# Gate and up products of 12 of 22 tiles by seven half-size products (Strassen, one level) on normalised x

## The chip, the cores and the metric

The kernel runs on 1 core of one Trainium2 chip. The metric is the device time of one execution in microseconds (us), the median of several runs. Five engines work side by side and meet at semaphores: PE (TensorE, matmuls), DVE (VectorE), ACT (ScalarE), POOL (GpSimd) and SP (SyncE, which issues the weight loads). Each engine works through its own program strictly in order.

## The reference, cut to what matters

A two-layer encoder trunk on x of 512 tokens by 1024 features, all in float32. It has four feed-forward blocks, and between them mixers (convolution and attention in layer 0, a short gated convolution in layer 1) that the change does not touch.

```
def rmsnorm(x, g):
    y = xf * lax.rsqrt(jnp.mean(xf * xf, axis=-1, keepdims=True) + EPS)
    return (y * g.astype(jnp.float32)).astype(x.dtype)

def swiglu(x, w_gate, w_up, w_down):
    return (jax.nn.silu(x @ w_gate) * (x @ w_up)) @ w_down

x = x + FFN_RES * swiglu(rmsnorm(x, ffn1_norm[layer]), ffn1_w_gate[layer],
                         ffn1_w_up[layer], ffn1_w_down[layer])
```

`w_gate` and `w_up` are 1024 x 2816, which is 22 tiles of 128 columns; `w_down` is 2816 x 1024.

## The kernel before

**Layout.** Activations are kept transposed: 128 features on the partitions, 512 tokens along the free dimension. x times the norm's gain is held as `xg_hi` and `xg_lo`, 8 feature tiles of 128 x 512 each. Every float32 operand is held as a high part (rounded to the matmul's float32r) and a low part (the rest), and one product is three matmuls: high by high, high by low, low by high (`product`, L1288 to 1292).

**A feed-forward block** is a "pair" phase and a "resid" phase (the product with `w_down`). The pair phase has 44 units: gate and up of tile 0, gate and up of tile 1, and so on. A unit is 8 products over the feature tiles into one PSUM bank, 24 matmuls of 128x128 by 128x512 (`projection`, L1305). Four units make a group; the units of a group use banks 0 to 3. Group 0 is written out, the others are a loop.

**What a unit needs.** SP loads its 512 KB into one of four `raw` slots. ACT copies it to `w_hi` (L637, one instruction over 128x1024) once the unit two before is finished on PE, because there are two `w_hi` and `w_lo` slots; DVE subtracts (L950) to make `w_lo`. The next load into a raw slot waits for the `w_lo` made from it.

**What a tile needs afterwards.** DVE multiplies the gate bank by `rstd` (L1025), ACT applies silu (L688), POOL multiplies by `rstd` again for the up side (L516), DVE multiplies by the up bank (L1032, `hid`), ACT copies to `h_hi` (L693), DVE subtracts to `h_lo` (L1035). The normalisation of x is thus applied to the products, not to x, and `rstd` is only computed while the first units run: PE sums the squares after unit 0, ACT takes a logarithm and an exponential, DVE finishes (L962 to 964).

**Order.** Nothing plans at run time. The order on each engine is what the functions named `pair` and `group` write out; an engine that waits holds up all that stands behind it.

Of the kernel before, what the change touches and what calls it, by code (L numbers as in the profile page):

```python
# [28 lines left out]
P = 128  # L29
BANKS = 8  # L30
EPS = 1e-6
MASKED = -1.0e30


# [15 lines left out]
def plan(phases):  # L50
    unit = pair = gate_act = h = 0
    for n, ph in enumerate(phases):
        ph.unit0, ph.pair0, ph.act0, ph.h0, ph.pair_end = unit, pair, gate_act, h, pair
        unit += ph.units
        if ph.kind == "pair":
            pair += ph.units // 2
            if ph.gate != "none":
                gate_act += ph.units // 2
            if ph.gate == "silu":
                h += ph.units // 2  # L60
        if n:
            phases[n - 1].next = ph
    return phases


def trunk(nc, t_in, out):
# [67 lines left out]
    raw = own("raw", [P, 4, SLOT])  # L134
    w_hi, w_lo = own("w_hi", [P, 2, SLOT], f32r), own("w_lo", [P, 2, SLOT], f32r)
    rstd = own("rstd", [P, S])
# [4 lines left out]
    hid = at("hid", [P, S], f32, HID)  # L141
    sq = own("sq", [P, 2, S])
    sq_sum = own("sq_sum", [P, S])
    cum = own("cum", [P, S])
    WIDE = 2 * P
# [21 lines left out]
    rough, corr = at("rough", [P, S], f32, ACTED), at("corr", [P, S], f32, ACTED + ROW)  # L167


    x_rows = at("x_rows", [P, TB, D], f32, H)  # L170
# [86 lines left out]
    NEXT_SPLIT = (12, 13, 16, 17)  # L257

    def every(t, offset, period, count):

        n = (t - offset) // period
        return n if t >= offset and (t - offset) % period == 0 and n < count else None
# [26 lines left out]
    with ExitStack() as ctx:  # L289
        bank = [ctx.enter_context(nc.psum_tensor(f"bank{i}", [P, S], f32)) for i in range(BANKS)]  # L290

        def sem(name):
# [20 lines left out]
        hhi_ready, hlo_ready = sem("hhi_ready"), sem("hlo_ready")  # L313
        step = sem("step")
        wf_cleared, wfhi_ready, wflo_ready, f_done = (
            sem("wf_cleared"), sem("wfhi_ready"), sem("wflo_ready"), sem("f_done"))
# [27 lines left out]

        block = ctx.enter_context(nc.Block())

        def gate_cols(tensor):
# [98 lines left out]
        def _(pool):  # L446
# [56 lines left out]
            def gates(ph):  # L503
# [4 lines left out]
                def one(f, par):  # L508
                    src = gate if ph.gate == "none" else acted
                    if ph.gate == "none":  # L510
                        pool.wait_ge(gate_scaled, f + (ph.pair0 + 1))
# [8 lines left out]
                if ph is A_GATE:  # L520
                    for f in range(2, n):
# [92 lines left out]
        def _(act):  # L614
# [4 lines left out]
            def split_hi(ph, g, u):  # L619
# [7 lines left out]
                if isinstance(g, int):  # L627
                    act.wait_ge(w_arrived[u % 4], 16 * (i // 4 + 1))
                    if ph.kind == "out" and i - ph.unit0 >= 2:
                        act.wait_ge(unit_done, i - 3)  # L630
                    elif i >= 2:
# [27 lines left out]
            def head_root(n):  # L659
# [3 lines left out]
                act.activation(bank[4 + n][0:2 * HEADS, :], h_rough[:, :], ACT.Square).then_inc(qk_root, 1)  # L663

            def pair(ph):
                def group(g):
                    first = isinstance(g, int) and g == 0
                    for u in range(4):
                        f, par = g * 2 + u // 2, u // 2
                        if not (first and u in (1, 2)):  # L670
                            split_hi(ph, g, u + 2)
# [11 lines left out]
                        if u % 2 == 0 and ph.gate != "none":  # L683
                            func = ACT.Silu if ph.gate == "silu" else ACT.Sigmoid
                            act.wait_ge(gate_scaled, f + (ph.pair0 + 1))
                            if not first:
                                act.wait_ge(gate_ready, f + (ph.pair0 - 1))
                            act.activation(acted[:, par, :], gate[:, par, :], func).then_inc(gate_acted, 1)  # L688
# [5 lines left out]

                run_groups(ph, group)

# [160 lines left out]
            for ph in phases:  # L857
# [11 lines left out]
                elif ph.kind == "qk":  # L869
# [4 lines left out]
                    for i in range(ph.units):  # L874
# [11 lines left out]
                        if i == CUM_AT:  # L886

                            act.wait_ge(cum_ready, 1)
                            act.wait_ge(gate_ready, A_GATE.pair0 + CB)
                            act.activation(cum_r[:, :], cum[:, :], ACT.Copy).then_inc(cumhi_ready, 1)  # L890
# [32 lines left out]
        def _(dve):  # L923
# [45 lines left out]
            def conv_taps(n, late=False):  # L969
# [24 lines left out]
                taps[0] += n  # L994

            def pair(ph):
                def group(g):
                    first = isinstance(g, int) and g == 0
                    for u in range(4):
                        f, half = g * 2 + u // 2, u // 2  # L1000
                        if ph is A_GATE and not first and u == 0:

# [3 lines left out]
                                              raws(gate_cols(wf_hi)), ALU.subtract).then_inc(wflo_ready, 1)  # L1006
                        if not (first and u in (1, 2)):
                            split_lo(ph, g, u + 2)
# [15 lines left out]
                        if u % 2 == 0:  # L1024
                            dve.tensor_tensor(gate[:, half, :], bank[u][:, :], rstd[:, :], ALU.mult)\  # L1025
                                .then_inc(gate_scaled, 1)
                            if ph is A_GATE:
                                conv_taps(TAPS_A[4 * g + u])
                            continue
                        dve.wait_ge(gate_ready, f + (ph.pair0 + 1))  # L1030
                        if ph.gate == "silu":
# [26 lines left out]

                run_groups(ph, group)

# [226 lines left out]
        def _(pe):  # L1287
            def product(dst, a, b, start, stop):  # L1288

                pe.matmul(dst, a[0], b[0], start=start, stop=False)  # L1290
                pe.matmul(dst, a[0], b[1], start=False, stop=False)  # L1291
                return pe.matmul(dst, a[1], b[0], start=False, stop=stop)  # L1292

# [11 lines left out]
            def projection(ph, g, u, wait_x=False, before=None):  # L1305
# [11 lines left out]
                last.then_inc(unit_done, 1)  # L1317

            def pair(ph):
                def group(g):  # L1320
                    first = isinstance(g, int) and g == 0
                    for u in range(4):
                        if not first:

                            pe.wait_ge((gate_scaled, pair_out)[u % 2], g * 2 + (ph.pair0 + u // 2 - 1))
                        hook = None
# [20 lines left out]

                run_groups(ph, group)

# [204 lines left out]
            for ph in phases:  # L1554
# [6 lines left out]
                elif ph.kind == "single":  # L1561
                    for i in range(ph.units):
                        if i >= 4:
                            pe.wait_ge(y_out, i - 3)
                        else:

                            pe.wait_ge((gate_scaled, pair_out)[i % 2], ph.pair_end - 1 + i // 2)
                        projection(ph, i // 4, i % 4)
                elif ph.kind == "qk":
# [7 lines left out]
                    for i in range(ph.units):  # L1577
                        if i >= 4:
                            pe.wait_ge(qk_out, i - 3)
                        else:  # L1580
                            pe.wait_ge((gate_scaled, pair_out)[i % 2], A_GATE.pair0 + CB - 1 + i // 2)
                        projection(ph, i // 4, i % 4)
# [51 lines left out]
```

## Time and profile before

| | |
|---|---|
| median of 3 runs | 1889.01 us (1888.88 to 1891.73) |
| the profiled execution's own time | 1889.06 us |
| its span, first to last instruction | 1887.3 us |
| mean granted TensorE clock | 0.997 of full speed |
| PE busy | 1865.3 us |
| DVE busy | 841.8 us |
| ACT busy | 656.8 us |
| POOL busy | 365.9 us |

The busy time of PE counts pipelined matmuls whose ends are modelled, so overlapping matmuls show a longer duration (0.39 us) than the distance between their starts. For PE's pace read the starts; for the other engines a duration runs until the result is written, and the next independent instruction can start a little before that.

### The profile page before, as it was taken

What the parts mean: (1) busy time and instruction counts of PE and PEld (TensorE: products, weight loads), DVE (VectorE), ACT (ScalarE), POOL (GpSimd) and SP (SyncE); (2) the same over time, 40 slices, a digit from 0 to 9 for tenths busy, and PEclk for the clock granted to TensorE, in tenths of its full rate; (3) what the DMA queues carried; (4) which work ended last, traced back from release to release, by engine and by line L of the source; (5) the groups of instructions that cost most, each with busy time, mean ns of one, the idle gap of its engine ahead of it and who ended that gap; (6) DMA issues with size and microseconds to landing.
All of it is one profiled execution on the core that took longest, in us unless ns stands there. A gap on an engine that the chain in (4) does not pass through costs nothing.

```text
span 1887.3 us, 22491 instructions
## 1 busy us (share of the span) xinstructions
PE 1865.3 (99%) x8333; PEld 1523.6 (81%) x8333; DVE 841.8 (45%) x969; ACT 656.8 (35%) x851; POOL 365.9 (19%) x317
## 2 busy tenths in 40 slices
PE   8999999999989999999999999999999999999999
PEld 6888888887568888888888888888888888888887
DVE  5433433377776534333434344333455444344321
ACT  5333332246866433332224333322312343333221
POOL 3111111139883211110111111101113121111000
PEclk9999999999999999999999999999999999999999
DMA  5333343332102333333323333433233333333331
GB/s 158 92 98 100 93 119 92 86 82 76 33 7 85 100 100 92 97 108 108 92 82 89 100 100 89 121 93 99 78 96 94 101 91 99 100 91 106 109 113 38
DMA packets 341404, 174.86 MB, mean 93 GB/s; under 512 B 6304, under 2 KB 340332, under 8 KB 341356
## 3 DMA queue, kind: packets, MB, share of 16 engines
q1 hardware_dynamic: 337100, 172.12, 31.6%
q10 hardware_dynamic: 4256, 2.11, 0.4%
q8 instruction: 30, 0.49, 0.1%
q14 instruction: 18, 0.15, 0.0%
HBM read 172.10 MB, written 2.10 MB: 92 GB/s over the span
## 4 chain that ended last, share of the span: by engine, by line
PE 91%; POOL 3%; DVE 2%; ACT 2%; issue 1%; DMA 0%; SPq 0%; ACTq 0%; POOLq 0%
PE bank L1290 30%; PE bank L1291 30%; PE bank L1292 30%; POOL conv L499 2%; DVE w_lo L950 1%; POOL probs_a L594 0%; ACT w_hi L637 0%; DVE conv L986 0%; DMA x_rows<-in_x 0%; PE bank L1353 0%; DVE pt_lo L1189 0%; PE bank L1538 0%; PE bank L1488 0%; ACT tap_prod L770 0%; DVE neg_max L1196 0%
## 5 line engine op out<-in xcount | busy, mean ns | idle before, releaser
L950 DVE TENSOR_TENSOR w_lo<-raw,w_hi 128x1024 fp32r<-128x1024 f32 (+2 forms) x308 | 407.1, 1323 | 734.9 <-ACT w_hi L637 734.5
L1290 PE MATMUL bank<-xg_hi,w_hi 128*128 128x512 f32 x1728 | 677.0, 392 | 3.3 <-DVE w_lo L950 2.7
L1292 PE MATMUL bank<-xg_hi,w_lo 128*128 128x512 f32 x1728 | 672.9, 389 | 0.0
L1291 PE MATMUL bank<-xg_lo,w_hi 128*128 128x512 f32 x1728 | 672.8, 389 | 0.0
L637 ACT ACTIVATE w_hi<-raw 128x1024 fp32r<-128x1024 f32 (+2 forms) x308 | 340.1, 1104 | 767.6 <-PE bank L1292 767.4
L1290 PEld LDWEIGHTS bank<-xg_hi,w_hi 128*128 128x128 f32 x1728 | 324.6, 188 | 78.0 <-issue 5.2
L1291 PEld LDWEIGHTS bank<-xg_lo,w_hi 128*128 128x128 f32 x1728 | 324.7, 188 | 68.4 <-issue 1.4
L1292 PEld LDWEIGHTS bank<-xg_hi,w_lo 128*128 128x128 f32 x1728 | 324.6, 188 | 67.3
L516 POOL TENSOR_TENSOR scaled<-acted,rstd 128x512 f32<-128x512 f32 x92 | 118.8, 1291 | 860.8 <-ACT acted L688 849.3
L1290 PE MATMUL bank<-h_hi,w_hi 128*128 128x512 f32 x704 | 274.4, 390 | 0.0
L1292 PE MATMUL bank<-h_hi,w_lo 128*128 128x512 f32 x704 | 274.0, 389 | 0.0
L1291 PE MATMUL bank<-h_lo,w_hi 128*128 128x512 f32 x704 | 273.9, 389 | 0.0
L483 POOL TENSOR_TENSOR sq_sum<-sq_sum,sq 128x512 f32<-128x512 f32 x48 | 76.3, 1590 | 421.6 <-ACT sq L647 420.3
L1292 PEld LDWEIGHTS bank<-h_hi,w_lo 128*128 128x128 f32 x704 | 132.1, 188 | 27.6
L1290 PEld LDWEIGHTS bank<-h_hi,w_hi 128*128 128x128 f32 x704 | 132.2, 188 | 27.4
L1291 PEld LDWEIGHTS bank<-h_lo,w_hi 128*128 128x128 f32 x704 | 132.2, 188 | 27.0
L688 ACT ACTIVATE acted<-gate 128x512 f32<-128x512 f32 x92 | 58.2, 633 | 192.0 <-DVE gate L1025 192.0
L693 ACT ACTIVATE h_hi<-hid 128x512 f32 (+1 forms) x88 | 55.7, 633 | 178.0 <-DVE hid L1032 178.0
L1035 DVE TENSOR_TENSOR h_lo<-hid,h_hi 128x512 f32 (+1 forms) x88 | 61.0, 693 | 78.1 <-ACT h_hi L693 78.1
L499 POOL TENSOR_TENSOR conv<-conv,tap_prod 128x511 f32<-128x511 f32 (+29 forms) x60 | 81.2, 1353 | 14.4 <-ACT tap_prod L770 7.3
L1077 DVE SCALAR_TENSOR_TENSOR x<-bank,x 128x512 f32<-128x512 f32 (+1 forms) x32 | 22.1, 692 | 127.3 <-PE bank L1292 127.3
L1025 DVE TENSOR_TENSOR gate<-bank,rstd 128x512 f32<-128x512 f32 x100 | 68.4, 684 | 0.2
(192 smaller groups left out, 1127.9 us busy)
## 6 DMA issues: line engine op xcount, KB each, us to landing
raw<-in_ffn_w_gate SPq DMA_DIRECT2D x88, 512.0 KB, 3.8
raw<-in_ffn_w_up SPq DMA_DIRECT2D x88, 512.0 KB, 3.8
raw<-in_ffn_w_down SPq DMA_DIRECT2D x64, 704.0 KB, 4.5
raw<-in_od_w_in SPq DMA_DIRECT2D x24, 512.0 KB, 3.8
raw<-in_ev_w_in SPq DMA_DIRECT2D x20, 512.0 KB, 3.8
raw<-in_ev_w_out SPq DMA_DIRECT2D x16, 256.0 KB, 2.8
raw<-in_od_w_out SPq DMA_DIRECT2D x8, 512.0 KB, 3.8
x_rows<-in_x SPq DMA_DIRECT2D x4, 512.0 KB, 6.8
```

Of the source, the lines that this page charges most:

```text
L483: pool.tensor_tensor(sq_sum[:, :], sq_sum[:, :], sq[:, half, :], ALU.add)\
L499: pool.tensor_tensor(conv[:, b, shift:S], conv[:, b, shift:S], tap_prod[:, p % NPROD, 0:S - shift], ALU.add).then_inc(tap_added, 1)
L516: pool.tensor_tensor(scaled[:, :], src[:, par, :], rstd[:, :], ALU.mult).then_inc(gate_ready, 1)
L637: act.activation(w_hi[:, u % 2, c0:c0 + n], raw[:, u % 4, 0:n], ACT.Copy).then_inc(whi_ready, 1)
L688: act.activation(acted[:, par, :], gate[:, par, :], func).then_inc(gate_acted, 1)
L693: act.activation(h_hi[:, bass.ds(f, 1), :], hid[:, :], ACT.Copy).then_inc(hhi_ready, 1)
L950: dve.tensor_tensor(w_lo[:, u % 2, c0:c0 + n], raw[:, u % 4, 0:n], raws(w_hi[:, u % 2, c0:c0 + n]), ALU.subtract).then_inc(wlo_ready, 1)
L1025: dve.tensor_tensor(gate[:, half, :], bank[u][:, :], rstd[:, :], ALU.mult)\
L1035: dve.tensor_tensor(h_lo[:, one, :], hid[:, :].unsqueeze(1), raws(h_hi[:, one, :]), ALU.subtract).then_inc(hlo_ready, 1)
L1290: pe.matmul(dst, a[0], b[0], start=start, stop=False)
L1291: pe.matmul(dst, a[0], b[1], start=False, stop=False)
L1292: return pe.matmul(dst, a[1], b[0], start=False, stop=stop)
```

## The change

In each of the four feed-forward blocks, the tiles 4 to 15 (12 of 22) are computed another way. For one tile the two products x·gate and x·up form one 2x2 block product: x is cut into two halves of features (4 tiles of 128 each, `HK`) and two halves of tokens (256 each, `HT`), and the weights into four blocks, gate and up by the two halves of features (`b11`, `b21`, `b12`, `b22`). Strassen's scheme (in Winograd's form) needs seven half-size products of sums and differences instead of eight. Each half-size product is 4 products of three matmuls 128x128 by 128x256, 12 matmuls, so a tile is 84 matmuls over 256 columns where it was 48 over 512.

- **Operands of x.** The products need normalised x, so DVE makes `xn` (x times gain times `rstd`) during the tiles 0 to 3, POOL makes the four sums `s1` to `s4`, and ACT and DVE split seven quarters into high and low (`quad_high`, `quad_low`, 128x1024 each). Four quarters are then copied by POOL over `xg_hi` and `xg_lo` (8 copies), since their room in `h` is needed for the tiles' results.
- **Operands of the weights.** Per tile DVE makes four differences of blocks (`mix`: t1, t3, t2, t4), and ACT and DVE split seven blocks of 128x512 (`block_high`, `block_low`) into a ring of 5 places that takes the room of `w_hi` and `w_lo`. The split for product n waits until product n − 5 is finished on PE.
- **After the products.** ACT keeps three intermediate half banks per tile (`keep`: p1, p7, p6), DVE adds (`second_up`, `join_gate`), silu reads `gate`, and DVE multiplies in two halves (`hidden`). POOL has no work per tile.
- **Tiles 16 to 21** (`tail`) go as before, but on normalised x, without the two multiplications by `rstd`.
- The loops of the pair phase are written out for the feed-forward blocks; the loads on SP are unchanged. Tiles 0 to 3 are computed as before.

The core of the diff. PE's order, and the waits of the products that wait for more than their operands:

```diff
+            def p1(ph, f):
+                if f == FOLD0:
+                    pe.wait_ge(quad_lo, 8 * ph.fold + 7)
+                if f == FOLD0 + 2:
+                    pe.wait_ge(quad_moved, 8 * (ph.fold + 1))
+                pe.wait_ge(pair_out, ph.pair0 + f - 1)
+                folded_product(ph, "p1", f, "a11", True, True)
+            def p6(ph, f):
+                pe.wait_ge(p1_kept, FOLDS * ph.fold + f - FOLD0 + 1)
+            def p5(ph, f):
+                pe.wait_ge(u2_kept, FOLDS * ph.fold + f - FOLD0 + 1)
+            def p3(ph, f):
+                pe.wait_ge(up2_ready, FOLDS * ph.fold + f - FOLD0 + 1)
...
+                for f in range(FOLD0, FOLD1 - 1):
+                    p1(ph, f + 1)
+                    p5(ph, f)
+                    p7_(ph, f + 1)
+                    p2(ph, f)
+                    p6(ph, f + 1)
+                    p3(ph, f)
+                    p4(ph, f + 1)
```

ACT's split of a block, and ACT's order for one tile:

```diff
+            def block_high(ph, block, f):
+                n = fold_order(PRODUCT[block], f)
...
+                if n < RING:
+                    act.wait_ge(unit_done, ph.unit0 + 2 * FOLD0 - (1 if n < 2 else 0))
+                else:
+                    wait_product(act, ph, n - RING)
+                done = whi_ready if block in ("b21", "b22") else shi_ready
+                act.activation(ring_hi[:, n % RING, :], block_raw(block, f), ACT.Copy).then_inc(done, 1)
...
+                for f in range(FOLD0, FOLD1 - 1):
+                    block_high(ph, "t2", f + 1)
+                    if f > FOLD0:
+                        hidden_high(ph, f - 1)
+                    block_high(ph, "b22", f)
+                    keep(ph, f + 1, "p1")
+                    block_high(ph, "t4", f + 1)
+                    if f + 2 < FOLD1:
+                        block_high(ph, "b11", f + 2)
+                    keep(ph, f + 1, "p7")
+                    block_high(ph, "t1", f + 1)
+                    if f + 2 < FOLD1:
+                        block_high(ph, "t3", f + 2)
+                    gate_silu(ph, f)
+                    keep(ph, f + 1, "p6")
+                    block_high(ph, "b21", f + 1)
```

DVE's order for one tile:

```diff
+                for f in range(FOLD0, FOLD1 - 1):
+                    block_low(ph, "t2", f + 1)
+                    mix(ph, "t4", f + 1)
+                    if f > FOLD0:
+                        hidden_low(ph, f - 1)
+                    block_low(ph, "b22", f)
+                    block_low(ph, "t4", f + 1)
+                    second_up(ph, f)
+                    if f + 2 < FOLD1:
+                        block_low(ph, "b11", f + 2)
+                    block_low(ph, "t1", f + 1)
+                    if f + 2 < FOLD1:
+                        mix(ph, "t1", f + 2)
+                        mix(ph, "t3", f + 2)
+                    join_gate(ph, f)
+                    if f + 2 < FOLD1:
+                        mix(ph, "t2", f + 2)
+                        block_low(ph, "t3", f + 2)
+                    block_low(ph, "b21", f + 1)
+                    hidden(ph, f)
```

`mix` works in DVE with `dve.tensor_tensor(block_raw(name, f), block_raw(one, f), block_raw(other, f), ALU.subtract)`; t1 waits until both loads of the tile have arrived, t3 and t2 wait for t1. `join_gate` writes `gate` from a bank and the kept part over 128x512 and ends with `gate_scaled`; `gate_silu` waits for it. `hidden` waits for `gate_acted` and ends with `pair_out`:

```diff
+                    dve.tensor_tensor(hid[:, HT:S], up2[:, :], acted[:, f % 2, HT:S], ALU.mult)
+                    dve.tensor_tensor(hid[:, 0:HT], up[:, 0:HT], acted[:, f % 2, 0:HT], ALU.mult).then_inc(pair_out, 1)
```

Before tile 4, in the group of the tiles 2 and 3, per unit: DVE's `normalise` (in tiles 1 and 2: eight in all) and the seven quarters.

```diff
+                            for name in ((), ("a11", "a22"), ("a12", "s1"), ("s2", "s4", "s3"))[u]:
+                                quad_low(ph, name)
+                        if fold and g == 1 and u == 2:
+                            for name in ("t1", "t3", "t2"):
+                                mix(ph, name, FOLD0)
+                        if fold and g == 1 and u >= 2:
+                            if u == 3:
+                                block_low(ph, "b11", FOLD0)
+                                block_low(ph, "t3", FOLD0)
```

POOL, after its work for the tiles 0 and 1:

```diff
+                    pool.wait_ge(xn_ready, 12 * e + KD)
+                    pool.tensor_tensor(s1, c, d, ALU.add).then_inc(sum_ready, 1)
+                    one(2, 0)
+                    pool.wait_ge(sum_ready, 4 * e + 1)
+                    pool.tensor_tensor(s2, s1, a, ALU.subtract).then_inc(sum_ready, 1)
+                    pool.wait_ge(sum_ready, 4 * e + 2)
+                    pool.tensor_tensor(s4, b, s2, ALU.subtract).then_inc(sum_ready, 1)
+                    pool.tensor_tensor(s3, a, c, ALU.subtract).then_inc(sum_ready, 1)
+                    one(3, 1)
```

## Rows read from the trace of the kernel before

**Rows 1.** The page: busy time of each engine, and the chain that ended last.

```profile
PE 1865.3 (99%) x8333; PEld 1523.6 (81%) x8333; DVE 841.8 (45%) x969; ACT 656.8 (35%) x851; POOL 365.9 (19%) x317
...
PE 91%; POOL 3%; DVE 2%; ACT 2%; issue 1%; DMA 0%; SPq 0%; ACTq 0%; POOLq 0%
```

**Rows 2.** Timeline of ACT in a pair phase: start, duration, what.

```profile
101.01 1.06 ACT L637 ACTIVATE w_hi<-raw 128x1024 fp32r<-128x1024 f32 x1 [1.76 <-PE bank L1292]
...
106.45 1.06 ACT L637 ACTIVATE w_hi<-raw 128x1024 fp32r<-128x1024 f32 x1 [1.85 <-PE bank L1292]
```

**Rows 3.** Timeline of PE at the same place, across a unit's end.

```profile
100.58 0.39 PE L1292 MATMUL bank<-xg_hi,w_lo 128*128 128x512 f32 x1
100.81 0.39 PE L1290 MATMUL bank<-xg_hi,w_hi 128*128 128x512 f32 x1
```

**Rows 4.** Timeline of PE in the attention: twelve matmuls over 256 columns, their successor.

```profile
549.56 0.29 PE L1290 MATMUL bank<-pt_hi,v_hi 128*128 128x256 f32 x1
...
551.00 0.54 PE L1488 MATMUL bank<-ident,probs_b 128*128 128x128 f32 x2
```

**Rows 5.** Groups of DVE by shape: a 128x512 subtraction in SBUF.

```profile
L1035 DVE TENSOR_TENSOR h_lo<-hid,h_hi 128x512 f32 x72 | 49.9, 693 | 66.9 <-ACT h_hi L693 66.9
```

**Rows 6.** Timeline of DVE, 390 to 412 us, in written-out groups.

```profile
391.39 1.23 DVE L950 TENSOR_TENSOR w_lo<-raw,w_hi 128x1024 fp32r<-128x1024 f32 x1 [4.52 <-ACT w_hi L637]
392.53 0.68 DVE L962 TENSOR_TENSOR corr<-rough 128x512 f32<-128x512 f32 x1
393.25 0.69 DVE L963 SCALAR_TENSOR_TENSOR corr<-corr,mean_sq 128x512 f32<-128x512 f32 x1
...
406.24 0.68 DVE L1039 TENSOR_TENSOR a_in<-bank,scaled 128x512 f32<-128x512 f32 x1
406.85 3.07 DVE L986 SCALAR_TENSOR_TENSOR conv<-bank,conv_w,conv 128x505 f32<-128x505 f32 x4
409.83 0.41 DVE L1004 TENSOR_TENSOR wf_lo<-wf_raw,wf_hi 128x256 fp32r<-128x256 f32 x1
410.17 1.22 DVE L950 TENSOR_TENSOR w_lo<-raw,w_hi 128x1024 fp32r<-128x1024 f32 x1
```

**Rows 7.** Timeline of ACT, 386 to 400 us.

```profile
390.29 1.06 ACT L637 ACTIVATE w_hi<-raw 128x1024 fp32r<-128x1024 f32 x1 [0.82 <-PE bank L1292]
...
395.43 0.64 ACT L688 ACTIVATE acted<-gate 128x512 f32<-128x512 f32 x1 [2.77 <-DVE gate L1025]
395.96 1.05 ACT L637 ACTIVATE w_hi<-raw 128x1024 fp32r<-128x1024 f32 x1
```

**Rows 8.** Timeline in the attention: two ACT copies of 256 columns from PSUM.

```profile
549.92 0.66 ACT L819 ACTIVATE pt_hi<-bank 128x256 fp32r<-128x256 f32 x2
```

**Rows 9.** Timeline of PE in the attention: first matmuls after a wait.

```profile
552.89 0.36 PE L1290 MATMUL bank<-pt_hi,v_hi 128*128 128x256 f32 x1
553.09 0.28 PE L1291 MATMUL bank<-pt_lo,v_hi 128*128 128x256 f32 x1
```

**Rows 10.** DMA issues: KB each, median us from issue to landing.

```profile
raw<-in_ffn_w_up SPq DMA_DIRECT2D x18, 512.0 KB, 3.8
```

**Rows 11.** Timeline of PE, start of the third feed-forward block, after unit 0.

```profile
989.75 1.02 PE L1353 MATMUL bank<-sq_sum,ones 128*128 128x512 f32 x2
```

**Rows 12.** Timeline of DVE there.

```profile
1000.76 0.69 DVE L1025 TENSOR_TENSOR gate<-bank,rstd 128x512 f32<-128x512 f32 x1
1003.10 1.52 DVE L950 TENSOR_TENSOR w_lo<-raw,w_hi 128x1024 fp32r<-128x1024 f32 x1 [1.65 <-ACT w_hi L637]
```

**Rows 13.** Timeline of POOL there.

```profile
1002.25 1.29 POOL L516 TENSOR_TENSOR scaled<-acted,rstd 128x512 f32<-128x512 f32 x1 [13.56 <-ACT acted L688]
```

**Rows 14.** Groups of DVE by shape: the scale-and-subtract over 128x512.

```profile
L957 DVE SCALAR_TENSOR_TENSOR xg_lo<-x,vec,xg_hi 128x512 fp32r<-128x512 f32 x28 | 31.2, 1114 | 1.8 <-ACT xg_hi L645 1.6
```

**Rows 15.** Windows of 2 us in the attention: busy times of the engines, granted clock.

```profile
524.00:526.00 2.00, 0.75 (x5) 0.51 (x6) 1.68 (x6) 2.00 (x8) 2.00 (x3) 1.00 0.00 0
...
528.00:530.00 2.00, 1.68 (x7) 1.01 (x6) 1.45 (x5) 1.52 (x6) 2.00 (x3) 0.50 0.03 8
```

More of the change, by code:

```diff
@@ L32 @@
 MASKED = -1.0e30
+FOLD0, FOLD1 = 4, 16
 class Phase:
@@ L50, in plan @@
 def plan(phases):
-    unit = pair = gate_act = h = 0
+    unit = pair = gate_act = h = scaled = ready = folds = 0
     for n, ph in enumerate(phases):
         ph.unit0, ph.pair0, ph.act0, ph.h0, ph.pair_end = unit, pair, gate_act, h, pair
+        ph.scaled0, ph.ready0, ph.fold = scaled, ready, folds
         unit += ph.units
         if ph.kind == "pair":
+            scaled += FOLD1 if ph.gate == "silu" else ph.units // 2
+            ready += FOLD0 if ph.gate == "silu" else ph.units // 2
+            folds += ph.gate == "silu"
             pair += ph.units // 2
@@ L257, in trunk, with fold_order, fold_count, mix_count @@
     NEXT_SPLIT = (12, 13, 16, 17)
+    FOLDS = FOLD1 - FOLD0
+    BLOCK = {"p1": "b11", "p7": "t3", "p6": "t2", "p4": "t4", "p5": "t1", "p2": "b21", "p3": "b22"}
+    PRODUCT = {b: p_ for p_, b in BLOCK.items()}
+    def fold_order(name, f):
+        n = f - FOLD0
+        if name in ("p1", "p7", "p6", "p4"):
+            first = ("p1", "p7", "p6", "p4").index(name)
+            return first if n == 0 else 4 + 7 * (n - 1) + 2 * first
+        last = ("p5", "p2", "p3").index(name)
+        return 4 + 7 * n + (2 * last + 1 if n < FOLDS - 1 else last)
+    FOLD_ORDER = sorted((fold_order(name, f), name, f) for name in BLOCK for f in range(FOLD0, FOLD1))
+    assert [n for n, _, _ in FOLD_ORDER] == list(range(7 * FOLDS))
+    def fold_count(n):
+        return sum(name not in ("p2", "p3") for _, name, _ in FOLD_ORDER[:n + 1])
+    def mix_count(ph, name, f):
+        return 4 * (FOLDS * ph.fold + f - FOLD0) + ("t1", "t3", "t2", "t4").index(name) + 1
     def every(t, offset, period, count):
@@ L665, in pair, with tail @@
+            def tail(ph):
+                for f in range(FOLD1, KF):
+                    split_hi(ph, f // 2, f % 2 * 2 + 2)
+                    gate_silu(ph, f)
+                    split_hi(ph, f // 2, f % 2 * 2 + 3)
+                    hidden_high(ph, f)
             def pair(ph):
+                fold = ph.gate == "silu"
                 def group(g):
@@ L996, in pair, with tail @@
+            def tail(ph):
+                for f in range(FOLD1, KF):
+                    split_lo(ph, f // 2, f % 2 * 2 + 2)
+                    split_lo(ph, f // 2, f % 2 * 2 + 3)
+                    hidden(ph, f)
+                    hidden_low(ph, f)
             def pair(ph):
+                fold = ph.gate == "silu"
                 def group(g):
@@ L1346, in group @@
                             sum_squares(ph)
-                run_groups(ph, group)
+                if ph.gate == "silu":
+                    group(0)
+                    group(1)
+                    folded(ph)
+                    tail(ph)
+                else:
+                    run_groups(ph, group)
             def sum_squares(ph):
```

330 lines of the change are left out of this document (310 added, 20 removed).

## The prediction

> **What bounds the kernel now.** I read the page first: PE is busy 99% of the span and holds 91% of the chain that ended last; DVE and ACT are busy 45% and 35% [rows 1]. So PE's pace is the time, and I read it from starts. In a pair phase ACT's split of the weights starts each time a unit has ended, at 101.01 and 106.45: a unit is 5.44 us, a tile 10.88, a matmul over 512 columns 0.227 [rows 2, 3]. ACT starts 0.20 after the start of the next unit's first matmul (100.81): this is how late an engine learns that PE is through [rows 2, 3]. Nothing else is on the path in these phases, so a change that saves PE work helps only as long as DVE and ACT deliver operands and clear banks at the new pace.
>
> **PE's own work.** The trace has matmuls over 256 columns in the attention: twelve and the start of their successor take 1.44 us, 0.120 each, at full clock [rows 4]. That is exactly the length of one new product. A folded tile is 84 x 0.120 = 10.1 us instead of 10.88. The saving is thus 0.8 us a tile, not an eighth of 10.88, since 256 columns cost more than half of 512. If nothing ever waited, 48 tiles would save 38 us.
>
> (The Trainium skill, "TensorE: Matmul & The Clock Gate", Back-to-back issue gap, gives N/2.4 + 2.5 ns, 109 ns at 256 columns; by it a product is 1.31 us and a folded tile 9.2. The rows say 0.120, the measurement decides; what limits the forecast below is another engine by either figure.)
>
> **DVE and ACT per tile.** Prices: a 128x512 operation of DVE lasts 0.69 [rows 5]; the next independent one starts 0.60 to 0.61 after its start (406.24 to 406.85), the next that needs its result 0.72 after (392.53 to 393.25), and after one of 256 columns the next starts 0.34 later, its own duration being 0.41 [rows 6]. ACT: a start every 0.53 behind a 128x512 operation of 0.63 [rows 7], and every 0.28 behind a copy of 256 columns from PSUM (two in 0.66, one being 0.38) [rows 8]. From ACT's end to DVE's start it is 0.04 (390.29 + 1.06 = 391.35, start 391.39) [rows 6, 7]. DVE gets per tile 7 `block_low`, 4 `mix`, `join_gate`, `hidden_low` and three half operations: 13 x 0.60 + 3 x 0.34 + three dependent starts at 0.12 = 9.2 us. That fits in 10.1 with 0.9 to spare, if it never waits. It must wait.
>
> **The loop that sets the pace.** The ring holds 5 operands, so a split starts only when the product five before is finished; DVE's order is fixed, with `hidden(f)` last; and p1(f+2) uses the banks of tile f and waits for `pair_out` of `hidden(f)`. This closes a circle from p1(f+1) to p1(f+2). With 0 at the start of p1(f+1):
> p1(f+1), p5(f), p7(f+1), p2(f) run to 4 x 1.44 = 5.76. ACT may split t1(f+1), five places after p2(f), at 5.96, done 6.59. DVE: `block_low` t1 at 6.63, `mix` t1(f+2) at 7.35, `mix` t3 (needs t1) at 8.07, `join_gate(f)` at 8.67, ended 9.36. Meanwhile ACT has split t3(f+2) (8.80 to 9.33) and starts silu at 9.40, keeps p6 at 9.93, splits b21(f+1) from 10.21 to 10.84. DVE has done `mix` t2 and `block_low` t3 by 10.5 and idles; `block_low` b21 at 10.88, the two halves of `hidden(f)` at 11.48 and 11.82, ended 12.23. PE restarts about 0.1 later: its first matmul after a wait is followed after 0.20 instead of 0.12 [rows 9]. So p1(f+2) starts at 12.3, while PE was ready at 10.1: 2.2 us of idle per tile, and a cycle of 12.3 against 10.88.
> The earlier part of DVE's list doesn't matter: t2, `mix` t4, `hidden_low`, b22, t4, `second_up` and b11 end at 5.8 at the latest, each gated by ACT and by PE's products 0 to 2. The load of the up block of f+2 waits for `block_low` b22(f), ended 3.0; with some 0.2 to the issue and 3.8 to land [rows 10] it arrives at 7.0, just before `mix` t1 at 7.35: hidden, with 0.3 to spare. Bounds of the cycle: if ACT's detour over silu, p6 and b21 is hidden altogether, `block_low` b21 starts at 10.47 and the cycle is 11.9; if each of the seven operations of DVE in the circle costs its full 0.69, it is 0.7 more, 13.0. I take 12.3, since all its prices are starts of the same shapes.
>
> **The entry.** Unit 1 of a block starts 0.43 after the sum of squares at 989.75 [rows 11], so units 1 to 7 end at 990.2 + 7 x 5.44 = 1028.3; there p1 of tile 4 could start. It waits for the seven quarters, all of which pass DVE. DVE's list from its split at 1003.10 [rows 12], in starts: three `gate` 1.8; three `hid` with `h_lo`, 1.98 each with ACT between, 5.9; four splits of 1.14 (391.39 to 392.53 [rows 6]) 4.6; eight `normalise` at 0.9, between 0.69 [rows 6] and 1.11 [rows 14], 7.2; seven `quad_low` at 1.14, 8.0; three `mix` 2.2; two `block_low` 1.2. Together 30.9. Three times it waits for ACT right behind it, with 1.06 for a quarter and once silu before it: 3.8. p1 starts at about 1037.8: 9.5 us of idle PE. Then p6 waits for `keep` p1, which in ACT stands behind `h_hi` of tile 3, t4 and b11, and these behind `hid`, `h_lo`, t2 and `mix` t4 in DVE: 4.9 us after p1's start at the earliest instead of 2.9, so 2.1. POOL's four sums over 1024 elements (1.29 for 512 [rows 13], so about 2.6 each) are late by less than DVE, but they slow it: its split beside POOL took 1.52 instead of 1.23 [rows 6, 12]. And after 9.5 us of idle the clock will be at 1.2 GHz: in the attention it stood at 0.50 of full speed from 528 on, after PE had been busy only 0.75 of 2 us at 524 [rows 15]. One product at half clock costs 1.44 more; most of it lies in the wait of p6, I add 1.0. Entry: 12.6, between 8 (half of the ACT waits and p6's wait gone, clock kept) and 18 (`normalise` at 1.11, each of some ten operations 0.3 longer beside POOL, the clock back two products later).
>
> **The sum.** The tiles 4 to 15 took 12 x 10.88 = 130.6. Now: entry 12.6; p1, p7, p6, p4 of tile 4 5.8; ten cycles from p1(5) to p1(15) 123; the seven products of the last 10.1; the last three 4.3; 1.0 at the exit, where the split of unit 32 waits for p5(15). Together 156.8, 26.2 more per block, 105 for four. Tiles 16 to 21 stay bound by PE (24 x 0.227 a unit), and the two operations less per tile lay beside PE: 0. The profiled execution took 1889.06 (span 1887.3 and 1.8 around it), the median 1889.01, so both bases give **1994 us**. With the bounds, 10 x 0.4 and 4.6 down and 10 x 0.7 and 5.4 up per block: 1960 to 2044.
>
> **The rivals.**
> *PE sets the pace, entry covered.* Busy sums speak for it: DVE's 9.2 is under 10.1. For it, 9.5 us of entry must also be found. 4 x 12 x 0.8 = 38 less: 1851. Against it stand the circle and the entry's list. (The Trainium skill, "Perfetto Trace Analysis", Identifying the Most-Contended Engine, says to optimise the engine of highest occupancy first; that is PE, and by that rule this would be the outcome. By busy share the trace agrees; the order of waits speaks against.)
> *PE sets the pace, the entry is paid.* If the circle closes under 10.1 (it would have to lose 2.2 of 12.3), the balance per block is 12.6 + 1.0 − 9.6 = +4: 1905.
> *The clock falls in every cycle.* PE idles 2.2 us in a stretch, each time. It fell in the attention behind a stretch with 1.25 of 2 us idle, and was still full in that stretch [rows 15], so one such gap is about what preceded the fall there; against it, PE here runs 10 us without a gap between them. Four products at half clock would lengthen the circle by 5.8; if half of them are hit, 2.9 x 40 = 116 more: 2110. It decides only if idle 18% of the time is enough.
> *It doesn't do what it says* is no case: 84 half matmuls replace 48 in the code.
>
> **How the numbers follow.** The main case 0.80, the clock 0.08, PE's pace with paid entry 0.07, with covered entry 0.05. From no change a measurement of this kernel tells about 0.2%. Faster 0.06 (the covered entry, and a corner of the paid one), the same 0.02, slower 0.92. The likeliest case's own range is 1960 to 2044; for 8 in 10 with the other cases' tails I give 1935 to 2070.
>
> **What would show it.** PE in a folded tile: p1 to p1 12.3 us, one gap of 2.2 before p1 ended by DVE's `hidden`, no other; 1.44 per product. DVE busy about 10.2 us (full durations) of 12.3, waiting for ACT before `block_low` t1 (about 0.8) and b21 (0.4). A gap of about 9.5 us before tile 4, ended by the last quarter's `quad_low` or `block_low` t3, and a second of 2 before p6; granted clock 0.5 only behind them. The pair phase 265 us instead of 239. I am wrong if p1's gap is missing or ended by another, if products take other than 1.44, or if the entry's gap is under 6.

## The result, and the profile after

| | before | after |
|---|---|---|
| median | 1890.37 us (1888.88 to 1892.23, 4 runs) | 2098.0 us (2095.29 to 2098.98, 4 runs) |
| ratio | | 1.1096, 95% interval 1.1076 to 1.1115 |
| profiled span | 1887.3 us | 2093.5 us |
| mean granted TensorE clock | 0.997 | 0.952 |

The change makes the kernel 11% slower: 208 us more where 105 were forecast, and above both ranges (1960 to 2044 for the likeliest case, 1935 to 2070 for 8 in 10). The sign, the place and the loop of the prediction hold; the clock inside the cycles and the size of the entry don't. The page after, against [rows 1] (busy time of the engines, the granted clock in tenths over 40 slices, the chain that ended last):

```profile
PE 1907.2 (91%) x10061; PEld 1641.8 (78%) x10061; DVE 1196.1 (57%) x1553; ACT 818.0 (39%) x1267; POOL 375.9 (18%) x293
...
PEclk9899999999999989999998899999999997999999
...
PE 72%; DVE 13%; ACT 6%; issue 6%; POOL 3%; DMA 0%; DVEq 0%; ACTq 0%; SPq 0%; POOLq 0%
```

PE went from 99% busy to 91%, and from 91% of the chain to 72%: DVE, ACT and "issue" have taken the rest. What PE waits for (engine, tile and line, what it waits for: us in total, times, longest):

```profile
PE bank L1676 <- DVE hid L1289: 79.1, 36, 2.2
PE bank L1676 <- DVE ring_lo L1229: 42.1, 4, 11.2
PE bank L1676 <- DVE w_lo L1178: 23.2, 7, 4.6
PE bank L1676 <- ACT part L807: 13.2, 4, 3.6
```

The first line is the forecast circle: 36 gaps before p1, each 2.2 us, ended by `hidden`. The second is the entry's gap before p1(4), the fourth that before p6. Four of the third's seven waits are a gap of 4.5 to 4.7 us before unit 7 that was not forecast.

**A cycle.** Timeline of PE after, third block, around one p1:

```profile
1183.91 0.28 PE L1678 MATMUL bank<-xg_hi,ring_lo 128*128 128x256 f32 x1
1186.39 0.39 PE L1676 MATMUL bank<-xg_hi,ring_hi 128*128 128x256 f32 x1 [2.20 <-DVE hid L1289]
1186.61 0.28 PE L1677 MATMUL bank<-xg_lo,ring_hi 128*128 128x256 f32 x1
...
1187.52 0.42 PE L1678 MATMUL bank<-xg_hi,ring_lo 128*128 128x256 f32 x1
1187.74 0.41 PE L1676 MATMUL bank<-xg_hi,ring_hi 128*128 128x256 f32 x1
...
1190.86 0.28 PE L1676 MATMUL bank<-s_hi,ring_hi 128*128 128x256 f32 x1
1190.98 0.28 PE L1677 MATMUL bank<-s_lo,ring_hi 128*128 128x256 f32 x1
```

Starts stand 0.12 apart right after the gap, then 0.21 to 0.22 for 3.4 us, then 0.12 again. Windows of the same stretch (busy us and instructions of PE, PEld, DVE, ACT, POOL; granted clock; DMA share, GB/s):

```profile
1184.40:1186.40 2.00, 0.01 (x1) 0.01 (x1) 1.71 (x5) 1.09 (x4) 0.00 (x0) 1.00 0.00 0
...
1187.40:1190.70 3.30, 3.30 (x17) 3.30 (x17) 1.62 (x3) 0.90 (x2) 0.00 (x0) 0.50 0.50 146
1190.70:1200.40 9.70, 7.51 (x63) 7.31 (x61) 7.00 (x13) 4.72 (x10) 0.00 (x0) 1.00 0.19 57
```

The clock falls to 1.2 GHz (0.50) 1 us after PE has resumed, and is back at 2.4 at 1190.70. From p1(6) to p1(15), the p1 of this block start at 1172.41, 1186.39, 1200.41, 1214.42, 1228.44, 1242.39, 1254.93, 1268.94, 1282.96 and 1296.96: eight cycles of 13.95 to 14.02 us and one of 12.54. The undisturbed one is what 12.3 was forecast for. In all four blocks 29 of these 36 cycles take 13.88 to 14.03 us, and 7 take 12.53 or 12.54.

**The entry.** DVE after, 1112 to 1153 us, by shape (count, busy us, mean ns, idle before):

```profile
L1262 DVE TENSOR_TENSOR a_lo<-xn,a_hi 128x1024 fp32r<-128x1024 f32 x3 | 8.1, 2711 | 1.1 <-ACT a_hi L796 1.1
L1262 DVE TENSOR_TENSOR s_lo<-s_sum,s_hi 128x1024 fp32r<-128x1024 f32 x4 | 6.6, 1691 | 1.6 <-ACT s_hi L796 1.6
L1178 DVE TENSOR_TENSOR w_lo<-raw,w_hi 128x1024 fp32r<-128x1024 f32 x2 | 4.6, 2292 | 0.3 <-ACT w_hi L745 0.3
...
L1412 DVE TENSOR_TENSOR hid<-bank,scaled 128x512 f32<-128x512 f32 x3 | 2.0, 675 | 0.0
```

A 128x1024 subtraction takes 1.23 us in [rows 6]; here it is up to 3.4 us (the timeline has `a_lo` 3.39 at 1130.78 and `w_lo` 3.36 at 1124.71), while an operation that takes one input from PSUM, `hid`, keeps its 0.68. POOL's timeline there:

```profile
1123.66 3.32 POOL L614 TENSOR_TENSOR s_sum<-s_sum,xn 128x1024 f32<-128x1024 f32 x1
1127.06 3.24 POOL L616 TENSOR_TENSOR s_sum<-xn,s_sum 128x1024 f32<-128x1024 f32 x1
1130.27 2.82 POOL L617 TENSOR_TENSOR s_sum<-xn 128x1024 f32<-128x1024 f32 x1
...
1139.79 2.03 POOL L625 CAST xg_hi<-a_hi 128x1024 fp32r<-128x1024 f32 x1
```

Two pairs of these rows say how the two engines meet. `w_lo` of 1124.71 ends at 1128.07, POOL's operation beside it at 1126.98; `a_lo` of 1130.78 ends at 1134.17, POOL's at 1133.09. Each time DVE is through 1.08 or 1.09 us after POOL, a little less than the 1.22 that it takes alone: it looks as if it had stood still until POOL had ended. (POOL's ends are rough in this profile.) The price is then not a fixed one but what is left of POOL's operation.

PE at the gaps of the entry and at its two ends, the sum of squares and the first matmul of the `w_down` phase (timeline, third block; in [rows 11] the sum of squares is at 989.75):

```profile
1089.98 1.02 PE L1843 MATMUL bank<-sq_sum,ones 128*128 128x512 f32 x2
...
1128.21 0.76 PE L1676 MATMUL bank<-xg_hi,w_hi 128*128 128x512 f32 x1 [4.53 <-DVE w_lo L1178]
...
1146.46 0.55 PE L1676 MATMUL bank<-a_hi,ring_hi 128*128 128x256 f32 x1 [10.45 <-DVE ring_lo L1229]
...
1154.58 0.58 PE L1676 MATMUL bank<-s_hi,ring_hi 128*128 128x256 f32 x1 [3.54 <-ACT part L807]
...
1377.08 0.39 PE L1676 MATMUL bank<-h_hi,w_hi 128*128 128x512 f32 x1
```

The same two ends before are [rows 11] and

```profile
1224.57 0.39 PE L1290 MATMUL bank<-h_hi,w_hi 128*128 128x512 f32 x1
```

so this stretch grew from 234.8 to 287.1 us, by 52.3. In the other blocks it is 49.9, 51.5 and 52.6: together 206.3, the whole difference of the spans (206.2). The time outside the pair phases of the feed-forward blocks is the same.

### The profile page after: what moved, and what is told of

It reads as the page before. It is cut to its first block, busy times and chain, and to the rows that moved or that the text cites. A ratio compares the mean times of both kernels' runs of the same rounds, so it can differ in the third digit from the quotient of the medians.

```text
span 2093.5 us, 26606 instructions
## 1 busy us (share of the span) xinstructions
PE 1907.2 (91%) x10061; PEld 1641.8 (78%) x10061; DVE 1196.1 (57%) x1553; ACT 818.0 (39%) x1267; POOL 375.9 (18%) x293
## 4 chain that ended last, share of the span: by engine, by line
PE 72%; DVE 13%; ACT 6%; issue 6%; POOL 3%; DMA 0%; DVEq 0%; ACTq 0%; SPq 0%; POOLq 0%
PE bank L1676 24%; PE bank L1677 23%; PE bank L1678 23%; POOL conv L584 2%; DVE w_lo L1178 2%; ACT ring_hi L785 2%; DVE gate L1277 1%; ACT acted L824 1%; DVE xn L1250 1%; DVE ring_lo L1229 1%; DVE s_lo L1262 1%; ACT w_hi L745 1%; DVE hid L1288 1%; DVE a_lo L1262 1%; DVE hid L1289 1%
## 5 line engine op out<-in xcount | busy, mean ns | idle before, releaser
L1676 PE MATMUL bank<-xg_hi,w_hi 128*128 128x512 f32 x960 | 382.6, 399 | 21.2 <-DVE w_lo L1178 20.9
L1677 PE MATMUL bank<-xg_lo,w_hi 128*128 128x512 f32 x960 | 377.4, 393 | 0.0
L1678 PE MATMUL bank<-xg_hi,w_lo 128*128 128x512 f32 x960 | 377.1, 393 | 0.0
L1676 PE MATMUL bank<-xg_hi,ring_hi 128*128 128x256 f32 x640 | 205.1, 321 | 88.4 <-DVE hid L1289 79.1
L1676 PEld LDWEIGHTS bank<-xg_hi,ring_hi 128*128 128x128 f32 x640 | 143.3, 224 | 96.4 <-DVE hid L1289 86.4
L1677 PE MATMUL bank<-xg_lo,ring_hi 128*128 128x256 f32 x640 | 201.0, 314 | 0.0
L1678 PE MATMUL bank<-xg_hi,ring_lo 128*128 128x256 f32 x640 | 200.5, 313 | 0.0
L1676 PE MATMUL bank<-s_hi,ring_hi 128*128 128x256 f32 x608 | 177.8, 292 | 13.4 <-ACT part L807 13.2
L1677 PE MATMUL bank<-s_lo,ring_hi 128*128 128x256 f32 x608 | 176.6, 290 | 0.0
L1678 PE MATMUL bank<-s_hi,ring_lo 128*128 128x256 f32 x608 | 176.2, 290 | 0.0
```

The source lines that it names most:

```text
L1676: pe.matmul(dst, a[0], b[0], start=start, stop=False, skip_group_check=again)
L1677: pe.matmul(dst, a[0], b[1], start=False, stop=False, skip_group_check=again)
L1678: return pe.matmul(dst, a[1], b[0], start=False, stop=stop, skip_group_check=again)
```

## The experiments

All are compared with the same kernel before (median 1889 to 1891 in each set). "After" is 2098.0.

**1. The order of the circle.** Only the order of instructions on DVE and ACT in a folded tile is changed:

```
 DVE     mix(ph, "t4", f + 1)
+        block_low(ph, "b22", f)
         if f > FOLD0: hidden_low(ph, f - 1)
-        block_low(ph, "b22", f)
 ...     block_low(ph, "b11", f + 2)
+        join_gate(ph, f)
         block_low(ph, "t1", f + 1)
         mix(ph, "t1", f + 2); mix(ph, "t3", f + 2)
-        join_gate(ph, f)
         mix(ph, "t2", f + 2)
+        hidden(ph, f)
         block_low(ph, "t3", f + 2)
         block_low(ph, "b21", f + 1)
-        hidden(ph, f)
 ACT     t1, silu, keep p6, t3, b21   (was t1, t3, silu, keep p6, b21)
```

> Only the order changes: DVE joins the gate before it splits t1 and multiplies hidden(f) before it splits t3 and b21; ACT applies silu right behind the split of t1. Theory A (a circle from p1 over the split of t1, join, silu, b21 and hidden back to p1 sets the cycle of the folded tiles, 12.5 us at full clock, and the clock's falls behind its gap add the rest up to the mean of 13.8): the circle is shorter than PE's own 10.1 us, so p1 to p1 becomes 10.1 to 10.6 us, the gap before p1 is under 0.5 us and the clock stays full in the cycles; four blocks times ten cycles times 3.4 us less: about 1960 us (1940 to 1985). Rival B (DVE's amount of work sets the cycle, its durations are 10.2 us and it waits in between): the order changes little, cycle 12 us or more, 2060 to 2100 us.

Measured 1982.7 us, ratio 1.0497 (1.0471 to 1.0523): 115 us less than after. In the third block p1(6) is at 1118.16 and p1(15) at 1215.94: 10.9 a cycle instead of 13.8, and no matmul among them runs at half pace, not even behind the two longest gaps, 1.45 and 1.62 us. So the circle holds; the time is inside the range and above the point expected. With the gaps the clock's falls went too, which experiment 2 puts at 46.8 of the 115 us. A wait of ACT for a load is new (waits, then the timeline of ACT, then PE's next p1):

```profile
ACT ring_hi L785 <- DMA raw<-in_ffn_w_gate: 50.4, 36, 2.7
```

```profile
1189.48 0.63 ACT L785 ACTIVATE ring_hi<-raw 128x512 fp32r<-128x512 f32 x1 [2.65 <-DMA raw<-in_ffn_w_gate]
```

```profile
1194.91 0.39 PE L1676 MATMUL bank<-xg_hi,ring_hi 128*128 128x256 f32 x1 [1.62 <-DVE hid L1289]
```

**2. The clock in the cycles.** After, with PE kept at work in the gap before p1 of the tiles 6 to 15; the products only write a bank that nobody reads:

```
+ def fill(n):
+     for _ in range(n):
+         pe.matmul(bank[5][:, 0:2 * P], ident_r[:, :], mask_r[:, 0:2 * P], start=True, stop=True)
  def p1(ph, f):
+     if f > FOLD0 + 1: fill(16)
```

> Order as in the change, but PE fills 1.9 of the 2.4 us before p1 of tiles 6 to 15 with 16 matmuls of 256 columns into a bank that nothing reads. Theory A (the clock falls because PE idles there): every cycle takes the 12.5 us that undisturbed ones take, no stretch at 1.2 GHz inside the cycles; 9 to 10 cycles of 1.3 us less per block: about 2048 us (2040 to 2060). Rival C (the clock falls for another reason, for instance the many short matmuls, or falls at all after the entry): the stretches stay, 2090 to 2110 us.

Measured 2051.2 us, ratio 1.0853 (1.0835 to 1.0871): PE does 640 matmuls more and the kernel is 46.8 us faster. PE's timeline, around a p1:

```profile
1177.67 2.08 PE L1725 MATMUL bank<-mask_r,ident_r 128*128 128x256 f32 x16
1180.03 0.39 PE L1676 MATMUL bank<-xg_hi,ring_hi 128*128 128x256 f32 x1 [0.28 <-DVE hid L1289]
```

From p1(6) at 1154.99 to p1(15) at 1267.76 they follow at 12.50 to 12.54 us, every one. This is the loop's own length, still set by DVE; the 1.5 us that most cycles took beyond it was the clock.

**3. The clock at the entry too.** On top of 2, 80 such matmuls before p1(4) and 20 before its p6.

> As the kernel that fills the cycles, and 80 more such matmuls (9.6 us) before p1 of tile 4 and 20 (2.4 us) before its p6, where PE idles at the entry. Theory A: the first products after the entry run at full clock too, worth up to 5 us per block besides: about 2030 us (2020 to 2045). If what follows the entry waits for DVE and ACT anyway, the clock there is hidden and it is the same as with the cycles alone, about 2048 us.

Measured 2049.2 us, ratio 1.0844 (1.0826 to 1.0862): 2 us less, 0.5 per block and within the spread, although the mean granted clock rose from 0.974 to 0.990. The 20 matmuls do not cover the whole wait for p6: PE still idles 2.6 us there. In the second and third block the clock falls behind that wait all the same, in the first and the last it stays full through the entry. From p1(4) to p1(6) the two blocks at full clock take 24.5 and 25.1 us, the other two 25.1 each. In the four blocks of the kernel after it is 24.9 to 26.3, and 26.0 in the third, where p6 and p4 take 5.3 for 2.9. So the half clock before p6 costs nothing, since p6 starts 8.1 us after p1(4) in all of them, and of what it costs behind p6 about 1 us per block is on the path, near the forecast's 1.0. Two blocks at full clock are thin evidence for this size.

**4. No POOL beside DVE in the entry.** After, with the four sums on DVE and the eight copies on ACT, all of them in the tile 4 (ACT):

```
- pool.tensor_tensor(s1, c, d, ALU.add) ...                 (and s2, s4, s3)
- pool.tensor_copy(whole[:, ks, ts], raws(quad[name][n][:, :, :]))      (8 of them)
+ dve.tensor_tensor(s1, c, d, ALU.add) ...                  (in group 1, before its first gate)
+ act.activation((xg_hi, xg_lo)[n % 2][:, ks, ts], raws(quad[name][n % 2][:, :, :]), ACT.Copy)
```

> Order as in the change, but the four sums of the entry are made by DVE instead of POOL and the eight copies over xg by ACT. Theory A (DVE's operations at the entry take 2 to 3 times their time because POOL works beside them): DVE's quarter splits fall from about 3.3 us to 1.23 us and the small ones from 1.5 to 0.69; although DVE gets 4.6 us more to do, p1 of tile 4 starts 5 to 9 us earlier: about 2070 us (2055 to 2080). Rival D (the entry is long because DVE's list is long, POOL's neighbourhood matters little): the four sums add 4.6 us per block and it becomes slower than the change, 2100 to 2118 us.

Measured 2077.5 us, ratio 1.0989 (1.0971 to 1.1008), in the range of theory A. DVE does 4.9 us of sums more per block, and yet its stretch is shorter. The same shapes of DVE in this kernel, 1112 to 1146 us:

```profile
L1288 DVE TENSOR_TENSOR s_lo<-s_sum,s_hi 128x1024 fp32r<-128x1024 f32 x4 | 4.9, 1272 | 1.6 <-ACT s_hi L779 1.6
L1288 DVE TENSOR_TENSOR a_lo<-xn,a_hi 128x1024 fp32r<-128x1024 f32 x3 | 3.6, 1220 | 0.3 <-ACT a_hi L779 0.3
```

From the sum of squares (1087.28) to p1(4) (1138.89) it is 51.6 us instead of 56.5; 48.0 was forecast, without the sums. So POOL's company had cost DVE about 9.8 there: the 4.9 gained and the 4.9 done in its place. The gap before p6 all but went (0.4 at the longest): p6 starts 5.35 us after p1(4), in the kernel after 8.12, where POOL's eight copies run beside DVE's `h_lo`, t2 and `mix` t4. What these two gained is partly lost again: the copies make ACT late, and p1(6) waits for the last of them, a wait that the experiment itself brought in:

```profile
PE bank L1704 <- ACT xg_lo L820: 21.4, 4, 5.8
```

**5. The load that was new in 1.** On top of 1, `hidden`, then b21, then t3 on both engines, and ACT keeps p7 before the split of b11, so that raw slots come free earlier.

```
 DVE     hidden(ph, f)
+        block_low(ph, "b21", f + 1)
         block_low(ph, "t3", f + 2)
-        block_low(ph, "b21", f + 1)
```

> On top of e1_order, DVE and ACT do hidden and block_low b21 ahead of t3, and ACT keeps p7 ahead of the split of b11, so that the buffers of the gate block's load come free earlier. In e1_order ring operand t1 waits 2.65 us for that load (50.4 us over 36 waits), and the tiles beside it take 11.96 us from join_gate to join_gate. If the load's late issue is what is left in the cycle: the wait is gone, a cycle takes 10.1 to 10.4 us, 4 x 10 x 1.3 to 1.6 less than the 1982.7 of e1_order, so about 1925 (1905 to 1945), with the entry unchanged at some 25 us per block. Rival: the load was only the last of several waits, the next one (DVE's chain through t1 and block_low) ends a few tenths of a us earlier, and the time stays at 1970 to 1985.

Measured 1981.7 us, ratio 1.0482 (1.0464 to 1.05): no change, as the rival had it. The wait for the load is gone from the list, but the nine cycles are now all 10.7. In 1 only two of the nine had been lengthened (11.74 and 11.95), the others took 10.47 to 10.67; I had taken one bad cycle for all. What is left before p1 is a wait of 0.4 for `hidden`, which stands behind a `mix` in DVE's order (timeline):

```profile
1178.25 0.69 DVE L1229 TENSOR_TENSOR ring_lo<-raw,ring_hi 128x512 fp32r<-128x512 f32 x1 [1.03 <-ACT ring_hi L785]
1178.86 0.68 DVE L1277 TENSOR_TENSOR gate<-bank,part 128x512 f32<-128x512 f32 x1
...
1181.61 0.69 DVE L1244 TENSOR_TENSOR mix<-raw,mix 128x512 f32<-128x512 f32 x1
1182.21 0.42 DVE L1288 TENSOR_TENSOR hid<-up,acted 128x256 f32<-128x256 f32 x1
```

**6. The entry rewritten.** On top of 5: sums on DVE between the other work, the quarters in the order in which the products need them, one wait for each instead of one for all, the copies on ACT over four tiles.

```
- QUADS = list(quad)                      + QUADS = ["a11", "s3", "s2", "a22", "s1", "a12", "s4"]
- if f == FOLD0: pe.wait_ge(quad_lo, 8 * ph.fold + 7)                       (in p1)
+ if f == FOLD0: pe.wait_ge(quad_lo, 8 * ph.fold + QUADS.index(operand) + 1)   (in each product)
- folded: reads xg from tile FOLD0 + 2    + from tile FOLD0 + 5
```

> On top of e6_order_load, the entry of each block is rewritten: the four quarter sums of x on DVE instead of POOL, interleaved with the normalisation in the order in which the seven products need them; each product of tile 4 waits only for its own operands; the copies of the quarters are on ACT, two per tile over tiles 4 to 7. If the entry's gaps (10.4 and 3.8 us and the one of 4.5 before unit 7) come from DVE beside POOL and from the one wait of tile 4 for the last quarter, about 5 us of the 25 per block stay: 80 us less than e6_order_load, 1850 (1835 to 1885), at which it would be faster than the kernel before. Rival: DVE's list itself is the entry's length (30 us of operations whoever does the sums), which leaves 12 to 15 per block: 1885 to 1905.

Measured 1926.1 us, ratio 1.0192 (1.0175 to 1.021): 55.6 us less than 5, 13.9 per block where 20 were expected. Both ranges had set out from the 1925 us expected of 5, which had measured 1981.7, so the time lies above them partly for that earlier miss. p1(4) now starts 40.1 after the sum of squares, 1.5 later than PE's own pace would have it, but PE's gaps of 11.0 and 3.8 became many of 0.6 to 2.6 in the tiles 4 and 5: from p1(4) to p1(6) eleven products of 1.44 take 24.7 us, 8.9 more than their own time, and the next three cycles 12.3, 11.0 and 11.1, before they are 10.7. In sum 12.6 of 26.1 us of entry stay in this block: the rival's "12 to 15", not the 5 of the main case. The waits (PE, in the order of the view):

```profile
PE bank L1792 <- DVE hid L1401: 26.9, 36, 3.1
PE bank L1792 <- DVE ring_lo L1262: 8.7, 6, 1.9
PE bank L1792 <- issue: 6.7, 8, 1.0
PE bank L1792 <- DVE w_lo L1211: 5.3, 4, 2.3
PE bank L1792 <- ACT part L791: 5.0, 4, 1.4
PE bank L1792 <- DVE up L1382: 3.9, 8, 0.8
```

The first line is p1's wait in every cycle, 0.4 in the steady ones, and with it the longest of the entry, 2.6 before p1(6) in the third block. Otherwise no single wait holds the entry any more: from p1(4) to that gap DVE is busy 19.8 of 22.1 us, ACT 12.9.

**7. `hidden` one place earlier.** On top of 6, DVE does `hidden(f)` before `mix` t2 of f + 2.

> On top of e7_entry, DVE computes hidden one mix earlier (before mix t2 instead of behind it). In e6_order_load and e7_entry a cycle is 10.73 us: p1 still waits 0.40 (0.55 from start to start more than the pace) for hidden, which DVE starts at 1182.21 right behind a mix, while the operands of hidden are there from 1180.20 on. If this is the last wait of the circle, hidden ends 0.60 earlier, the gap before p1 closes, the cycle is 10.1 to 10.3 and the eight steady tiles of a block save 0.45 to 0.6 each: 15 to 20 us less than the 1926 of e7_entry, about 1909 (1904 to 1914). Rival: DVE has only 1.0 us of slack in the cycle, the next place of the ring or the splits of t2 and b21 now end later, and the cycle stays at 10.6 to 10.8: 1920 to 1930.

Measured 1912.5 us, ratio 1.0122 (1.0105 to 1.0139): 13.6 us less and in the range. But the steady cycle fell from 10.73 to 10.48 only, between the two that were expected, and the gap before p1 to 0.15:

```profile
1129.83 0.42 DVE L1400 TENSOR_TENSOR hid<-up,acted 128x256 f32<-128x256 f32 x1
1130.17 0.42 DVE L1401 TENSOR_TENSOR hid<-bank,acted 128x256 f32<-128x256 f32 x1
1130.50 0.68 DVE L1277 TENSOR_TENSOR mix<-raw,mix 128x512 f32<-128x512 f32 x1
```

Of the 5.0 us that the third block saves, the six steady cycles give 1.5. The three behind p1(6), which took 12.3, 11.0 and 11.1, now take 10.5 each, 2.9 less, and 1.2 of this is the clock: it stood at 0.50 behind the gap of 2.6 us before p1(6), and stays at 1.00 behind the 2.0 us that are left. So the range was met partly by luck.

This is the best version tried. It is still 1.2% slower than before; none beat the kernel before.

**8. What half-size matmuls cost by themselves.** The kernel before, without any Strassen, each gate and up matmul of the groups from 1 on as two over 256 columns:

```
+ for cols in (slice(0, S // 2), slice(S // 2, S)):
+     for k in range(KD):
+         last = product(bank[u][:, cols], (wh[:, k, :], wl[:, k, :]),
+                        (xg_hi[:, k, cols], xg_lo[:, k, cols]), k == 0, k == KD - 1, again=True)
```

> The kernel before, in which each gate and up matmul over 512 columns of groups 1 and later of the feed-forward blocks is two over 256 (same weights twice, halves of the moving operand). Nothing else changes, and the result is the same. By the price of 0.120 us a unit is 48 x 0.120 = 5.76 instead of 5.44, 160 units x 0.32 = 51 us more: 1940 (1935 to 1946). Rival: the 0.120 holds for the attention's matmuls alone and a half costs half of 0.227, 0.113: no change, 1889 to 1895.

Measured 1941.5 us, ratio 1.0268 (1.0251 to 1.0286). ACT's splits, which follow the ends of units as in [rows 2]:

```profile
99.25 1.06 ACT L637 ACTIVATE w_hi<-raw 128x1024 fp32r<-128x1024 f32 x1 [2.10 <-PE bank L1292]
...
105.01 1.06 ACT L637 ACTIVATE w_hi<-raw 128x1024 fp32r<-128x1024 f32 x1 [2.08 <-PE bank L1292]
```

A unit is 5.76 instead of 5.44 us, so 48 matmuls of 256 columns are 0.120 each, as priced from the attention.

## Why the prediction was wrong

**Right: the circle.** The gap before each p1, 2.2 us, ended by `hidden`, with PE at 0.12 per matmul where the clock is full. DVE's chain stands in the order forecast; an undisturbed cycle is 12.53 (the mean of nine in experiment 2) against 12.3, 0.23 x 9 = 2.1 per block. Experiment 1 cut the loop by order alone and took 115 us off, the clock's share with it.

**Wrong: "granted clock 0.5 only behind them" (the entry's gaps), the clock held full in the cycles.** The prediction named the mechanism as a rival, priced it at 2.9 per cycle ("if half of them are hit", of four products), and gave it 0.08, because "PE here runs 10 us without a gap between them". 29 of 36 cycles have the fall. Its price is 1.5 each, half of what the rival took; experiment 2 gives 46.8 us for all, 11.7 per block. [rows 15] could not decide it. The prediction looked at the last stretch before the fall alone; in the three stretches before it PE idles too, 3.1 of 8 us in the four together (the same view; PE's busy time stands behind the comma):

```profile
518.00:520.00 2.00, 1.30 (x10) 0.67 (x6) 2.00 (x4) 0.36 (x1) 1.86 (x3) 1.00 0.00 0
520.00:522.00 2.00, 1.67 (x14) 1.28 (x16) 2.00 (x4) 1.09 (x3) 1.10 (x8) 1.00 0.00 0
522.00:524.00 2.00, 1.14 (x12) 0.80 (x12) 1.72 (x5) 1.31 (x5) 1.25 (x1) 1.00 0.00 0
```

So no row of the kernel before showed what a lone gap of 2.2 us does, for the rival or against it, and 0.08 was too sure. A fall in every cycle at 1.5 would have put the forecast at about 2054.

**Wrong: the size of the entry, "each of some ten operations 0.3 longer beside POOL", which even the upper bound of 18 took.** That 0.3 came from one row, a `w_lo` that met the last 0.44 us of a short operation of POOL [rows 6, 12, 13]: POOL ends at 1003.54 and `w_lo` at 1004.62, 1.08 later, the same distance as in the entry after. So the rows had it that DVE loses what is left of POOL's operation. Against POOL's sums of 2.8 to 3.3 us the same operation of DVE loses 2.1. p1(4) stands 56.5 after the sum of squares where 48.0 were forecast, 8.5 late; p1(6), behind p6 and the next cycle, 13.2 late. Of the further 4.7, 3.1 are p6's start, 8.1 after p1(4) where 5.0 were forecast: DVE beside POOL's copies is late with `mix` t4, and ACT has to split t4 before it keeps p1 (ACT's timeline in the kernel after has this split at 1153.11, after a wait of 4.08 us for the `mix`). Experiment 4, without POOL there, shows the cause for both parts. 1.4 are p6 and p4, 2.4 longer at half clock where the forecast added 1.0. This part is not the clock's alone: where experiment 3 kept it full, DVE and ACT were not ready, and the next cycle took 13.5 and 14.0 instead of 12.5. The rest is 0.2 in the cycle.

(The Trainium skill, "SBUF — State Buffer", SBUF: two separate sides, says that a DVE instruction with two SBUF inputs and a GpSimd one that reads SBUF exclude each other for a whole instruction. The rows agree: `a_lo` and `w_lo` with two SBUF inputs take 3.4 instead of 1.23, `hid` with one input in PSUM keeps 0.68. The prediction did not weigh it.)

**The sum.** Forecast for the third block 26.2, measured 52.3. The 26.1 between them: 8.5 before p1(4), 4.7 from there to p1(6), 13.9 in the nine cycles (124.6 instead of 110.7; 11.7 the clock, 2.1 the loop), less 1.0 that the exit did not cost. Four times this is the miss.

**The ceiling.** PE's own saving, 0.8 us a tile or 38 us, is confirmed (0.120 a matmul, 8). What costs is not PE's work but feeding it: seven `block_low`, four `mix` and the joins leave DVE 0.9 us of slack in 10.1 by the prediction's sum. In experiment 7 DVE is busy 9.2 of a cycle of 10.48 and waits 1.0 for ACT's split of b11. In experiment 7 the third block still takes 4.0 more than before: 1.6 before p1(4), 8.3 in the tiles 4 and 5 (24.1 for 15.8), 3.6 in the nine cycles and about 0.2 at the end, against 9.6 saved. (The Trainium skill, "Perfetto Trace Analysis", Identifying the Most-Contended Engine, says to optimise the engine of highest occupancy first, by which relieving PE would have paid. By these runs it did not: PE is still the busiest after, at 91%, and what helped was order and work on DVE, ACT and POOL, and in experiment 2 even more work for PE.) That a version faster than before exists was not shown. It would need the entry nearly free: moving the folded tiles later was not tried, since the quarters' room in `h` doesn't allow it.

## What to carry to other kernels

Before halving an engine's work, write down the loop of waits through the engines that feed it: if it is longer than the new pace, its order is the time, and changing the order adds no work. Count a regular gap of about 2 us in PE at full price plus 1.5 us for the clock behind it, until a run shows otherwise. Keep long POOL operations away from DVE operations with two inputs in SBUF where DVE is on the path, and let each product wait for its own operand, not for the last of a set.

## What the hardware showed that I had not expected

- With a gap of 2.2 us in each cycle of 12.5 us, PE being busy for the other 10.1, the clock fell to half for 3.4 us in 29 of 36 cycles. Sixteen matmuls without use in the gap pay for themselves (46.8 us).
- DVE's 128x1024 subtraction: 1.22 us alone, 2.71 on average over three beside POOL's sums, 3.4 at worst, and at its end 1.1 us after POOL's operation in the rows read.
- Half the columns are not half the time on PE: 0.120 for 256 against 0.227 for 512, 51 us over 160 units.
